# State tables and products in 64x64 blocks with later tables, and a 512-column product in the MLP's up units

## Chip, cores and metric

One core of one Trainium2 chip. The metric is the time of one execution on the device in microseconds (us); for the kernel before it is the median of three runs.

## The reference, cut to what matters

Two layers of a decoder trunk, one sequence of 256 tokens, model width 1024, all in float32.

```python
for l in range(DEPTH):                       # DEPTH = 2
    h = rmsnorm(x, norm_mix[l])
    u, sq, sk, sv, dq, dk, dv, gate_logits = jnp.split(h @ w_in[l], split_idx, axis=-1)
    y_ssm = jax.nn.gelu(s5_ssm(u, ...))      # 32 groups of 16 channels, 64 complex states each
    glu_a, glu_b = jnp.split(y_ssm @ ssm_w_glu[l], 2, axis=-1)
    y_ssm = glu_a * jax.nn.sigmoid(glu_b)
    ...                                      # stick-breaking and differential attention
    x = x + jnp.sum(gates * proj, axis=2) @ w_out[l]
    ...                                      # cross-attention into 256 memory tokens
    hm = rmsnorm(x, norm_mlp[l])
    x = x + jnp.square(jax.nn.relu(hm @ w_up[l])) @ w_down[l]      # hidden 4096

def s5_ssm(u, lam_re, lam_im, log_dt, b_re, b_im, c_re, c_im, d_skip):
    dt = exp(log_dt); lam_bar = exp(lam * dt); b_bar = (lam_bar - 1) / lam * b
    states = associative_scan(lam_bar, b_bar @ ug)      # over the 256 tokens
    return Re(c @ states) + d_skip * ug
```

## The kernel before, in words

**Weights.** All weights pass once, in 312 chunks of 128x1024 (512 KB), 156 a layer. SP loads them in order into seven slots; the load of chunk c waits until TensorE is done with chunk c - 7 (`load_chunk`). ScalarE copies each chunk to `w_hi` in the reduced type (L898, four slots), VectorE subtracts it from the original to `w_lo` (L1295, seven slots). A product is three matmuls that accumulate in PSUM (`three`, L1819 to L1821): high x high, high weight x low activation, low weight x high activation.

**Units.** Two chunks are a unit (`plan`): `u` 0 and 1, `sq` 2 and 3, `sk` 4 and 5, `sv` 6 and 7, `dq`, `dk`, `dv` 8 to 13, twelve gate units 14 to 25, then `glu`, `branch`, `wout`, cross-attention, and the MLP: `up` g (two units of 256 hidden columns), then `down` g-1. Kind "T" units keep the weights in the array and stream 256 columns of activations (48 matmuls); kind "N" units stream 512 columns of weights (24 matmuls). `unit_banks` gives each its PSUM banks; an `up` unit has one, T0 or T1, with its two blocks of 128 hidden columns side by side. ScalarE then takes the bank with relu, VectorE squares it, ScalarE and VectorE split it into `bT_hi`, `bT_lo` (`evac`).

**The order.** `side_stages` is a table written by hand: which other stages come after which unit. Every engine walks through units and stages in this same order and does its part; VectorE and ScalarE evacuate unit u, prepare the chunks of unit u + 2 (`prep`, before or after the stages by `DVE_PREP_EARLY` and its like), do `stage`, and last `later`. So an operation late on one of them holds all behind it.

**The state space.** 2048 states are 16 tiles (`STILES`) of 128 partitions; each tile has two groups of 64. Time is cut into 64 blocks of 4 steps. POOL (`tables`) makes powers of lam_bar (`product`, many operations on 128x16), zeroes the cross parts of `bN0` and `bN` (`zero_b`), and builds the phases in six doubling steps, then the decays. ScalarE gives the sine and cosine (`p_cos`), VectorE the reduced angle. VectorE multiplies them into C (`p_cv`) and B (`p_b0`, `p_bv`); because the two groups of a tile lie on different columns of a 128x128 block, the last sum of each runs once for each half of the partitions. TensorE makes `kt` from `bN0` and `ct` (`p_k`, L1931, and L1934 for the skip term), ScalarE copies it out in sixteen copies of 32 partitions; TensorE transposes `bN` (`p_bt`, L1804) and ScalarE copies it to `bt`. `p_k` follows unit 5, `p_bt` units 6 to 8. The input `u` is scaled by VectorE, goes to HBM and comes back turned (`turn_u`, at chunks 8, 10 and 12 of SP's order; the last part waits for `lam_made`). Then four times: `ssm_in` (TensorE L1963 into one bank, then eleven operations on VectorE with a scan), from unit 9 on (`FIRST`), and two units later `ssm_out` (L1977 and L1979, 128x128 weights, 64 columns). GELU follows at unit 15, its split at 18; `glu` (unit 26) needs it.
The tables of layer 1 are made in the same way beside layer 0's MLP, in `qk`, with the banks X0, X1.

**Beside it** run stick-breaking attention (`sb_s`, `sb_u`, `sb_p`, units 6 to 14, banks X0, X1, A3; matmuls on 64-row tiles at L1996 and L1998) and differential attention (`da_s`, `da_t`, `da_p`, from unit 16). For the first norm of layer 0 the kernel loads x transposed in two halves (`load_x_t`) and scales the result by the norm's factor afterwards (`row`, `r_row`), so the first products need no statistics.

## Time and profile before

| | |
|---|---|
| median of three runs | 1094.41 us (1093.07 to 1097.61) |
| profiled execution, its own time | 1096.48 us |
| its span | 1094.8 us, 18335 instructions |
| mean granted TensorE clock | 0.985 |
| HBM read | 172.87 MB |

The span is from the first to the last recorded instruction; the time has what lies around it too. An engine's busy time is the union of its instructions. A matmul's record is its latency: the next one starts long before it ends, so the distance between starts is what counts. In a timeline row, "x16" means that sixteen like instructions follow each other, and the second number is what they last together; in square brackets stands how long the engine was idle before, and what ended it.

### The profile page before, as it was taken

How to read it: one execution, taken by the hardware profiler on the slowest of the kernel's cores; microseconds unless marked ns; L12 is line 12 of the kernel's file. 1: busy time of each engine (PE TensorE's matmuls, PEld its weight loads, DVE VectorE, ACT ScalarE, POOL GpSimd, SP SyncE). 2: the span in 40 equal slices, each digit the busy share in tenths (PEclk: the TensorE clock that was granted, in tenths of full speed). 3: DMA queues.
4: the chain of work that ended last, by engine and by line, in shares of the span. 5: the costliest groups of instructions: out<-in, count | busy, mean ns of one | idle time of the engine just before them, and what ended most of it. 6: DMA issues, size and time to landing. Idle time of an engine off the chain costs nothing. (4 is left out here: it accounts for less than half of the span.)

```text
span 1094.8 us, 18335 instructions
## 1 busy us (share of the span) xinstructions
PE 1029.5 (94%) x7096; PEld 937.9 (86%) x7096; DVE 736.7 (67%) x1061; ACT 573.4 (52%) x868; POOL 176.7 (16%) x304
## 2 busy tenths in 40 slices
PE   5778999999999899999989999999999989999996
PEld 4766889989998799988979878998998979899995
DVE  4884975878875565887465579478787647555554
ACT  6446445546765555546554454554637546444442
POOL 5993300000000003997000011000000000000000
PEclk9889999999999999999999999999999999999998
DMA  7253336645554366654556543465565445666661
GB/s 281 97 173 95 98 120 194 201 141 174 176 175 149 96 232 182 189 172 136 172 173 189 163 130 97 135 213 154 155 181 175 146 135 160 190 189 192 182 188 74
DMA packets 58022, 177.21 MB, mean 162 GB/s; under 512 B 14160, under 2 KB 16208, under 8 KB 57680
## 3 DMA queue, kind: packets, MB, share of 16 engines
q1 hardware_dynamic: 57792, 176.04, 52.2%
q8 instruction: 57, 0.93, 0.3%
q14 instruction: 29, 0.24, 0.1%
q10 hardware_dynamic: 144, 0.00, 0.0%
HBM read 172.87 MB, written 3.15 MB: 161 GB/s over the span
## 5 line engine op out<-in xcount | busy, mean ns | idle before, releaser
L1295 DVE TENSOR_TENSOR s_w_lo<-s_raw,s_w_hi 128x1024 fp32r<-128x1024 f32 x312 | 377.3, 1238 | 146.7 <-ACT s_w_hi L898 143.0
L898 ACT ACTIVATE s_w_hi<-s_raw 128x1024 fp32r<-128x1024 f32 x312 | 321.0, 1054 | 215.2 <-PE p_T L1821 130.5
L1819 PE MATMUL p_T<-s_hT_hi,s_w_hi 128*128 128x256 f32 x1088 | 313.4, 288 | 12.0 <-DVE s_w_lo L1295 11.9
L1820 PE MATMUL p_T<-s_hT_lo,s_w_hi 128*128 128x256 f32 x1088 | 310.0, 285 | 0.0
L1821 PE MATMUL p_T<-s_hT_hi,s_w_lo 128*128 128x256 f32 x1088 | 309.7, 285 | 0.0
L1819 PEld LDWEIGHTS p_T<-s_hT_hi,s_w_hi 128*128 128x128 f32 x1088 | 210.7, 194 | 17.6 <-issue 16.2
L1820 PEld LDWEIGHTS p_T<-s_hT_lo,s_w_hi 128*128 128x128 f32 x1088 | 210.8, 194 | 0.4
L1821 PEld LDWEIGHTS p_T<-s_hT_hi,s_w_lo 128*128 128x128 f32 x1088 | 210.9, 194 | 0.0
L1819 PE MATMUL p_A<-s_w_hi,s_bT_hi 128*128 128x512 f32 x320 | 125.2, 391 | 2.4 <-DVE s_bT_lo L1295 2.4
L1820 PE MATMUL p_A<-s_w_lo,s_bT_hi 128*128 128x512 f32 x320 | 124.7, 390 | 0.0
L1821 PE MATMUL p_A<-s_w_hi,s_bT_lo 128*128 128x512 f32 x320 | 124.6, 389 | 0.0
L1819 PEld LDWEIGHTS p_A<-s_w_hi,s_bT_hi 128*128 128x128 f32 x320 | 60.1, 188 | 15.2 <-issue 3.2
L1821 PEld LDWEIGHTS p_A<-s_w_hi,s_bT_lo 128*128 128x128 f32 x320 | 60.1, 188 | 12.7
L1820 PEld LDWEIGHTS p_A<-s_w_lo,s_bT_hi 128*128 128x128 f32 x320 | 60.1, 188 | 11.7
L727 POOL TENSOR_TENSOR s_small<-s_small 128x16 f32<-128x16 f32 (+1 forms) x130 | 59.8, 483 | 10.2 <-ACT s_small L898 7.8
L1819 PE MATMUL p_T<-s_w_hi,s_hT_hi 128*128 128x512 f32 x128 | 52.2, 408 | 8.0 <-issue 8.0
L898 ACT ACTIVATE s_bT_hi<-s_att 128x512 fp32r<-128x512 f32 x32 | 20.2, 632 | 58.5 <-DVE s_att L1295 58.5
L1821 PE MATMUL p_T<-s_w_hi,s_hT_lo 128*128 128x512 f32 x128 | 50.8, 397 | 0.0
L1820 PE MATMUL p_T<-s_w_lo,s_hT_hi 128*128 128x512 f32 x128 | 50.7, 396 | 0.0
L727 POOL TENSOR_TENSOR s_small<-s_col,s_small 128x16 f32<-128x16 f32 x4 | 1.2, 313 | 296.7 <-ACT s_small L898 296.7
L1819 PE MATMUL p_A<-s_hT_hi,s_w_hi 128*128 128x256 f32 x128 | 37.8, 295 | 9.5 <-DVE s_hT_lo L1394 9.5
L1819 PE MATMUL p_T<-s_bT_hi,s_w_hi 128*128 128x256 f32 x160 | 45.9, 287 | 0.3 <-issue 0.3
(263 smaller groups left out, 1685.5 us busy)
## 6 DMA issues: line engine op xcount, KB each, us to landing
s_raw<-in_weights SPq DMA_DIRECT2D x312, 512.0 KB, 3.6
s_bt<-in_mem_t SPq DMA_DIRECT2D x2, 1024.0 KB, 6.1
s_st_y<-in_x_t SPq DMA_DIRECT2D x2, 512.0 KB, 6.9
s_x<-in_x SPq DMA_DIRECT2D x1, 1024.0 KB, 10.6
s_vN<-in_ssm_bc SPq DMA_DIRECT2D x2, 512.0 KB, 8.9
u_turn<-s_st_y SPq DMA_DIRECT2D x4, 256.0 KB, 3.8
s_uB<-u_turn SPq DMA_DIRECT2D x8, 128.0 KB, 3.4
s_bt<-in_mem SPq DMA_DIRECT2D x1, 1024.0 KB, 5.9
```

The lines of the kernel that those rows point to most:

```text
L727: return nc.gpsimd.tensor_tensor(o, i0, i1, op)
L898: return nc.scalar.activation(o, i, f, **kw)
L1295: return V.tensor_tensor(o, i0, i1, op)
L1819: mm(o, lhi, rhi, start=first, stop=False, **kw)
L1820: mm(o, lhi, rlo, start=False, stop=False, **kw)
L1821: return mm(o, llo, rhi, start=False, stop=last, **kw)
```

## The change

- `up` units: the high and low parts of the activations lie side by side in one tile `hT`. The high weight block streams both in one product of 512 columns into a whole bank, and the low weight block adds its 256 columns to the first half. A unit has two banks, T0 and T1 or X0 and X1. ScalarE copies the second halves, VectorE adds the first halves, and relu and square become one operation of VectorE.
- State space: each group has its own 64x64 block. `bt`, `ct`, `kt` are 64 columns wide; all their products are done as two products, on rows 0 to 63 and 64 to 127. The last sums of `p_cv`, `p_b0`, `p_bv` are one operation over all partitions; `bN` needs no zeroes. `p_bt` uses plain products with the identity in place of transposes. `p_k` has two products where one was (64 and 48 columns), and `kt` is copied in eight copies.
- Tables: POOL makes all angles in one operation, VectorE reduces them, ScalarE takes sine and cosine of all (also those of the rotary embedding); POOL makes the factors in fewer, wider operations. The phases are made by VectorE (`p_ph`), in units 9 to 11.
- Order in layer 0: the angles come before the statistics of the norm, which move behind unit 0; `row` moves behind unit 2. The tables begin two units later, the state stages at unit 13 (`FIRST`; 12 in layer 1). `turn_u` moves to chunks 16, 17 and 24, with eight transfers for four. x arrives in three parts. The memory tokens come later, and their transposed copy once instead of twice.

```diff
-FIRST = [9, 9]
+FIRST = [13, 12]
...
-    after(-1, "stats", "mix", 0)
-    after(-1, "stats", "mix", 1)
     if l == 0:
         after(-1, "p_angle", 0)
         after(-1, "p_cos", 0)
-        after(2, "lam", 0)
-        after(3, "lam", 1)
-        after(4, "p_params", 0)
-    after(1, "row")
+    for half in range(2):
+        after(-1 if l else 0, "stats", "mix", half)
+    if l == 0:
+        after(2, "put_u")
+        after(3, "lam_sum")
+        after(4, "lam_exp")
+        after(5, "lam")
+        after(13, "p_params", 0)
+    after(1 if l else 2, "row")
...
-        for n in range(8):
-            after(u["bt"][n // 2], "p_bt", tgt, n)
+        for n in range(4):
+            after(u["bt"][n], "p_bt", tgt, n)
+        for k in range(TAB_STEPS):
+            after(u["ph"][max(0, k - 3)], "p_ph", tgt, k)
     if l == 0:
-        pre(0, dict(ct=0, cv=(1, 2), b0=3, bv=(4, 5), k=(5, 6), bt=(6, 7, 7, 8)))
+        pre(0, dict(ct=-1, cv=(3, 4), b0=5, bv=(6, 8), k=(6, 7), bt=(8, 8, 10, 10), ph=(9, 10, 11)))
-        pre(1, dict(ct=up0 + 10, cv=(up0 + 12, up0 + 13), b0=up0 + 15, bv=(up0 + 16, up0 + 18),
-                    k=(up0 + 20, up0 + 21), bt=(up0 + 22, up0 + 23, up0 + 24, up0 + 25)))
+        pre(1, dict(ct=up0 + 10, cv=(up0 + 12, up0 + 13), b0=up0 + 14, bv=(up0 + 16, up0 + 17),
+                    ph=(up0 + 18, up0 + 19, up0 + 20), k=(up0 + 20, up0 + 21),
+                    bt=(up0 + 24, up0 + 25, up0 + 28, up0 + 29)))
...
-DVE_PREP_EARLY = set(range(0, 5)) | set(range(AT_UNIT["up", 0, 0], NU))
+DVE_PREP_EARLY = set(range(0, 6)) | set(range(AT_UNIT["up", 0, 0], NU))
...
-        return ["T0", "T1"][key[2]:][:1]
+        return ["T0", "T1"] if key[2] == 0 else ["X0", "X1"]
...
-        hT_hi, hT_lo = sb("hT_hi", [P, KD, T], F32R), sb("hT_lo", [P, KD, T], F32R)
+        hT = sb("hT", [P, KD, 2, T], F32R)
+        hT_hi, hT_lo = hT[:, :, 0, :], hT[:, :, 1, :]
...
-                    if c in (8, 10, 12):
-                        turn_u(l, c // 2 - 4, st)
+                    if c in (16, 17, 24):
+                        turn_u(l, (16, 17, 24).index(c), st)
...
-                    if l == 0 and c == 2 * AT_UNIT[("gate", 2), 0]:
+                    if l == 0 and c == 2 * AT_UNIT[("gate", 0), 0]:
                         sp.wait_ge(*st.at(s_ready, KB))
                         load(mem_raw, a["mem"][0].rearrange("(t p) d -> p t d", p=P), rows_landed)
-                    if c == 2 * AT_UNIT[("gate", 0), 0]:
-                        sp.wait_ge(*st.at(s_ready, KB))
-                        load(mem_t, a["mem_t"], mem_landed)
+                        load(mem_t[:, :, :], a["mem_t"], mem_landed)
...
+            nc.gpsimd.memset(kt[:, :, :], 0.0).then_inc(zeroed, 1)
+            nc.gpsimd.memset(bN0[:, :, :, :], 0.0).then_inc(zeroed, 1)
...
-            nc.gpsimd.memset(ct[:, :, :, :], 0.0).then_inc(zeroed, 1)
-            nc.gpsimd.memset(kt[:, :, :], 0.0).then_inc(zeroed, 1)
...
+                tt(TH[:, 1:1 + TAB_STEPS, :], TH[:, 0:1, :].broadcast_to([P, TAB_STEPS, STILES]),
+                   consts[:, 0:TAB_STEPS].unsqueeze(2).broadcast_to([P, TAB_STEPS, STILES]))\
+                    .then_inc(*st.sig(theta_ready, t + 1))
...
+                        for i, part in enumerate(X_PARTS):
+                            if i != 1:
+                                prep_chunk(i // 2)
+                            act.wait_ge(*st.at(xt_landed[i], 1))
...
-                    for q in (2 * n, 2 * n + 1):
-                        for j in range(BL):
-                            rows = slice(32 * j, 32 * j + 32)
-                            ins = fn(every[rows, q, :, 32 * j:P], src[32 * q:32 * q + 32, :, 0:P - 32 * j])
-                            last = n and q == 3 and j == BL - 1
-                            ins.then_inc(*st.sig(*freed(l, b, use))) if last else ins.then_inc(*st.mid())
+                    every = kt[:, :, :].rearrange("p (m e) c -> p e m c", e=2)
+                    for h in range(2):
+                        o = PC * h
+                        src = bank[b][o + 32 * n:o + 32 * n + 32, :].rearrange("p (m c) -> p m c", c=PC)
+                        fn(every[o:o + 32, n, :, :], src).then_inc(*st.mid())
+                        ins = fn(every[o + 32:o + 64, n, :, 32:PC], src[:, :, 0:32])
+                        ins.then_inc(*st.sig(*freed(l, b, use))) if n and h else ins.then_inc(*st.mid())
...
-                        take(r_b[i], b[0], key, ACT.Relu)
+                        act.wait_ge(*st.at(chunk_done, 2 * u + 2))
+                        for j, bk in enumerate(b):
+                            ins = fn(r_b[i][:, j * T:j * T + T], bank[bk][:, T:2 * T])
+                            ins.then_inc(*st.sig(up_copied)) if j else ins.then_inc(*st.mid())
...
+                        if s in (("p_angle", 0), ("p_cos", 0)):
+                            prep_chunk(2 + (s[0] == "p_cos"))
+                            n_first = AHEAD
...
+                    reduce_angle(st, TH[:, 0:n, :], KK[:, 0:n, :], THR[:, 0:n, :])
+                    V.tensor_scalar(THR[:, 0:n, :], THR[:, 0:n, :], PI_SAFE, -PI_SAFE, ALU.min, ALU.max)\
+                     .then_inc(*st.sig(angle_ready))
...
+                def products(raw, r, f, n, o):
+                    q = [o[:, 1024 * i:1024 * i + n * STILES * GC].rearrange("p (n i c) -> p n i c", n=n, c=GC) for i in range(2)]
+                    for i, m in enumerate((r, 1 - r)):
+                        tt(q[i], raw[:, m, :, :].unsqueeze(1).broadcast_to([P, n, STILES, GC]),
+                           FACTORS[:, i, f:f + n, :].unsqueeze(3).broadcast_to([P, n, STILES, GC])).then_inc(*st.mid())
+                    dve.wait_ge(*st.mine())
+                    return q
...
+                    q = products(c_raw, r, 0, BL - 1, early(t))
+                    tt(ct[:, r, :, GC:PC].rearrange("p i (n c) -> p n i c", c=GC), q[0], q[1],
+                       ALU.subtract if r else ALU.add).then_inc(*st.sig(ct_ready))
...
+                    q = products(b_raw, r, 3, BL, st_y[:, :, :].rearrange("p r n -> p (r n)"))
+                    tt(bN[:, r].rearrange("p i j c -> p j i c"), q[0], q[1], ALU.add if r else ALU.subtract)\
+                        .then_inc(*st.sig(bv_ready))
...
-                    for h in range(2):
-                        rows = slice(STATES * h, STATES * h + STATES)
-                        o = ct[rows, r, :, :].rearrange("p i (n h c) -> p n i h c", n=BL, h=2)[:, 1:BL, :, h, :]
-                        ins = tt(o, q[0][rows], q[1][rows], ALU.subtract if r else ALU.add)
...
+                    n = 1 << k
+                    c = [TURN[:, r, 1 + k, :].unsqueeze(1).unsqueeze(3).broadcast_to([P, 2, STILES, n]) for r in range(2)]
+                    e, o = phase[:, :, :, 0:n], phase[:, :, :, n:2 * n]
+                    part = st_y[:, :, :].rearrange("p r n -> p (r n)")[:, 0:2 * STILES * n]\
+                        .rearrange("p (r i n) -> p r i n", r=2, n=n)
+                    tt(o, e, c[0]).then_inc(*st.mid())
+                    tt(part, e, c[1]).then_inc(*st.mid())
                     dve.wait_ge(*st.mine())
...
+                    tt(o[:, 0], o[:, 0], part[:, 1], ALU.subtract).then_inc(*st.mid())
+                    tt(o[:, 1], o[:, 1], part[:, 0], ALU.add).then_inc(*(st.sig(phase_ready) if k + 1 == TAB_STEPS else st.mid()))
...
-                        dve.wait_ge(*st.at(*freed(l, b[0], key)))
-                        tt(q_b[i], r_b[i], r_b[i]).then_inc(*st.sig(sq_made))
+                        dve.wait_ge(*st.at(up_copied, 2 * g + i + 1))
+                        for j, bk in enumerate(b):
+                            tt(r_b[i][:, j * T:j * T + T], r_b[i][:, j * T:j * T + T], bank[bk][:, 0:T], ALU.add)\
+                                .then_inc(*st.sig(*freed(l, bk, key)))
+                        dve.wait_ge(*st.mine())
+                        V.scalar_tensor_tensor(out=q_b[i], in0=r_b[i], scalar=0.0, in1=r_b[i], op0=ALU.max, op1=ALU.mult)\
+                         .then_inc(*st.sig(sq_made))
...
+                                if key[0] == "up":
+                                    o = bank[banks[ft]]
+                                    mm(o[:, :], wh[:, k, c], hT[:, ks, :, :].rearrange("p r n -> p (r n)"),
+                                       start=(half == 0 and k == 0), stop=False, skip_group_check=True)
+                                    ins = mm(o[:, 0:T], wl[:, k, c], hi[:, ks, :], start=False,
+                                             stop=(half == 1 and k == kt // 2 - 1), skip_group_check=True)
+                                    continue
...
+                        tiles = [(e, slice(PC * h, PC * h + PC), slice(PC * h + 32 * e, PC * h + 32 * e + 32), PC * h)
+                                 for e in range(2) for h in range(2)]
+                        for m in range(STILES // 2):
                             for r in range(2):
-                                for q in range(4):
-                                    mm(bank[b][c * q:c * q + c, n * P:n * P + P], bN0[:, r, 4 * n + q, :],
-                                       ct[:, r, 4 * n + q, :], start=(r == 0), stop=False, skip_group_check=True)
-                            for q in range(4):
-                                ins = mm(bank[b][c * q:c * q + c, n * P:n * P + c], ident[0:c, 0:c],
-                                         diag_d[:, 4 * n + q, :], start=False, stop=True, skip_group_check=True)
+                                for e, rows, out_rows, p in tiles:
+                                    mm(bank[b][out_rows, PC * m:PC * m + PC], bN0[rows, r, 2 * m + e, GC:3 * GC],
+                                       ct[rows, r, 2 * m + e, :], start=(r == 0), stop=False, skip_group_check=True)
+                                for e, rows, out_rows, p in tiles:
+                                    mm(bank[b][out_rows, PC * m + GC:PC * m + PC], bN0[rows, r, 2 * m + e, 0:2 * GC],
+                                       ct[rows, r, 2 * m + e, 0:PC - GC], start=False, stop=False, skip_group_check=True)
+                            for e, rows, out_rows, p in tiles:
+                                two = slice(p, p + 2 * GC)
+                                ins = mm(bank[b][out_rows, PC * m:PC * m + 2 * GC], ident[two, two],
+                                         diag_d[two, 2 * m + e, :], start=False, stop=True, skip_group_check=True)
...
+                        for q in range(8):
+                            for h in range(2):
+                                rows = slice(PC * h, PC * h + PC)
+                                ins = mm(bank[b][rows, q * PC:q * PC + PC],
+                                         bN[rows, r, 8 * k + q, :, :].rearrange("p j c -> p (j c)"), ident[rows, rows],
+                                         start=True, stop=True, skip_group_check=True)
...
-                                ins = mm(bank[b][:, c + 1:c + NB], bt[:, r, i, :], uB[:, i, 0:NB - 1],
-                                         start=True, stop=True)
+                                for rows in HALVES:
+                                    ins = mm(bank[b][rows, c + 1:c + NB], bt[rows, r, i, :], uB[rows, i, 0:NB - 1],
+                                             start=True, stop=True, skip_group_check=True)
...
-                                mm(bank[b][:, c:c + NB], ct[:, r, i, :], st_y[:, r, i * NB:i * NB + NB],
-                                   start=(r == 0), stop=False)
-                            ins = mm(bank[b][:, c:c + NB], kt[:, i, :], uB[:, i, :], start=False, stop=True)
+                                for rows in HALVES:
+                                    mm(bank[b][rows, c:c + NB], ct[rows, r, i, :], st_y[rows, r, i * NB:i * NB + NB],
+                                       start=(r == 0), stop=False, skip_group_check=True)
+                            for rows in HALVES:
+                                ins = mm(bank[b][rows, c:c + NB], kt[rows, i, :], uB[rows, i, :], start=False, stop=True,
+                                         skip_group_check=True)
```

## Rows read from the trace of the kernel before

**Rows 1.** The page, busy us, share of the span and instructions of each engine

```profile
PE 1029.5 (94%) x7096; PEld 937.9 (86%) x7096; DVE 736.7 (67%) x1061; ACT 573.4 (52%) x868; POOL 176.7 (16%) x304
```

**Rows 2.** Timeline of PE in layer 0's MLP: start, length, instruction

```profile
455.04 0.39 PE L1821 MATMUL p_A<-s_w_hi,s_bT_lo 128*128 128x512 f32 x1
455.27 0.28 PE L1819 MATMUL p_T<-s_hT_hi,s_w_hi 128*128 128x256 f32 x1
...
457.66 0.28 PE L1821 MATMUL p_T<-s_hT_hi,s_w_lo 128*128 128x256 f32 x1
```

**Rows 3.** Stretches: length, busy PE, PEld, DVE, ACT, POOL, granted clock, DMA share, GB/s

```profile
9.45:13.10 3.65, 3.65 (x17) 3.65 (x18) 3.19 (x7) 3.62 (x8) 0.64 (x3) 1.00 1.03 421
9.45:95.36 85.91, 64.15 (x476) 57.77 (x477) 62.06 (x98) 45.56 (x80) 68.85 (x130) 0.88 0.44 159
...
514.90:518.30 3.40, 3.40 (x18) 3.40 (x18) 2.88 (x3) 1.54 (x3) 0.19 (x2) 0.51 0.00 0
950.00:1050.00 100.00, 100.00 (x628) 90.80 (x627) 55.77 (x54) 47.08 (x55) 0.00 (x0) 1.00 0.62 189
```

**Rows 4.** Timeline of PE: products that waited, in layer 0

```profile
29.75 0.55 PE L1819 MATMUL p_T<-s_hT_hi,s_w_hi 128*128 128x256 f32 x1 [6.51 <-DVE s_w_lo L1295]
...
70.43 0.77 PE L1819 MATMUL p_T<-s_w_hi,s_hT_hi 128*128 128x512 f32 x1 [7.13 <-issue]
...
88.53 1.65 PE L2005 MATMUL p_X<-s_att,s_tri 128*128 128x384 f32 x2 [3.07 <-DVE s_att L1713]
...
513.47 0.74 PE L1804 MATMUL p_X<-s_ident,s_gates 128*128 128x128 f32 x5 [1.90 <-ACT s_kt L898]
```

**Rows 5.** Timeline of PE: products on part of the array, transposes, state products

```profile
60.16 0.64 PE L1931 MATMUL p_A<-s_ct,s_tmp 128*32 128x128 f32 x16
60.73 0.26 PE L1934 MATMUL p_A<-s_att,s_ident 32*32 32x32 f32 x8
60.93 0.64 PE L1931 MATMUL p_A<-s_ct,s_tmp 128*32 128x128 f32 x16
...
102.34 0.39 PE L1998 MATMUL p_X<-s_qk 64*128 64x128 f32 x4
102.66 1.09 PE L1804 MATMUL p_A<-s_ident,s_gates 128*128 128x128 f32 x8
...
132.00 0.61 PE L1977 MATMUL p_A<-s_st_y,s_ct 128*128 128x64 f32 x4
```

**Rows 6.** Groups by line and shape, PE: counts, busy us, mean ns

```profile
L1977 PE MATMUL p_A<-s_st_y,s_ct 128*128 128x64 f32 x128 | 19.5, 275 | 0.0
L1963 PE MATMUL p_A<-s_uB,s_bt 128*128 128x63 f32 x128 | 15.6, 275 | 0.0
...
L1979 PE MATMUL p_A<-s_uB,s_kt 128*128 128x64 f32 x64 | 12.4, 275 | 0.0
L1804 PE MATMUL p_A<-s_ident,s_gates 128*128 128x128 f32 x32 | 4.4, 276 | 1.5 <-ACT s_bt L898 1.5
```

**Rows 7.** Timeline of DVE between 28 and 71 us

```profile
28.30 2.46 DVE L1295 TENSOR_TENSOR s_w_lo<-s_raw,s_w_hi 128x1024 fp32r<-128x1024 f32 x2 [3.99 <-ACT s_w_hi L898]
...
31.31 2.15 DVE L1295 TENSOR_TENSOR s_st_y<-p_A,s_r_row 128x512 f32<-128x512 f32 x2
...
39.02 1.83 DVE L1295 TENSOR_TENSOR s_att<-s_vN,s_small 128x768 f32<-128x768 f32 x2 [3.23 <-POOL s_small L727]
40.88 1.94 DVE L1295 TENSOR_TENSOR s_ct<-s_att 64x768 f32<-64x768 f32 x2
...
64.32 2.69 DVE L1295 TENSOR_TENSOR s_att<-s_vN,s_small 128x1024 f32<-128x1024 f32 x2
67.04 2.56 DVE L1295 TENSOR_TENSOR s_gates<-s_att 64x1024 f32<-64x1024 f32 x2
69.63 0.69 DVE L1535 SCALAR_TENSOR_TENSOR s_qk<-p_T,s_r_row 128x512 f32<-128x512 f32 x1
```

**Rows 8.** Timeline of ACT in layer 0's MLP

```profile
509.71 3.61 ACT L898 ACTIVATE s_kt<-p_X 32x512 f32<-32x512 f32 x8
```

More of the change, by code:

```diff
@@ L469, in hybrid_trunk @@
         x_landed = counted("x_landed", 1, step=16)
-        xt_landed = [counted(f"xt_landed{i}", 1, step=16) for i in range(2)]
+        xt_landed = [counted(f"xt_landed{i}", 1, step=16) for i in range(3)]
         lam_landed = counted("lam_landed", 1, step=16)
@@ L771, in product @@
-                def product(o, f, g, n):
-                    part = [small[:, 29 + 2 * i:29 + 2 * i + n, :] for i in range(4)]
-                    tt(part[0], f[0], g[0]).then_inc(*st.mid())
-                    tt(part[1], f[1], g[1]).then_inc(*st.mid())
-                    tt(part[2], f[0], g[1]).then_inc(*st.mid())
-                    tt(part[3], f[1], g[0]).then_inc(*st.mid())
-                    pool.wait_ge(*st.mine())
-                    tt(o[0], part[0], part[1], ALU.subtract).then_inc(*st.mid())
-                    tt(o[1], part[2], part[3], ALU.add).then_inc(*st.mid())
-                    pool.wait_ge(*st.mine())
@@ L1383, in row, with put_u @@
                     dve.wait_ge(*st.mine())
+                def put_u():
+                    dve.wait_ge(*st.at(chunk_done, 2 * AT_UNIT["u", 1] + 2))
+                    for i, bk in enumerate(("A0", "A2")):
+                        tt(by_block(u_flat[:, 512 * i:512 * i + 512]), by_place(bank[bk][:, :]),
+                           by_place(r_row[:, :]).broadcast_to([P, 2, BL, NB])).then_inc(*st.sig(*freed(l, bk, ("u", i))))
                 def norm(which):
@@ L1389, in norm @@
                     if which == "mix" and l == 0:
-                        for half in range(2):
-                            prep_chunk(half)
-                            for k in range(4 * half, 4 * half + 4):
+                        rope_angles()
+                        for i, part in enumerate(X_PARTS):
+                            if i != 1:
+                                prep_chunk(i // 2)
+                            for k in range(part.start, part.stop):
                                 dve.wait_ge(*st.at(norm_hi, k + 1))
@@ L1608, in stage @@
                         p_params(s[1])
-                    elif kind == "lam":
-                        lambdas(s[1])
+                    elif kind in ("lam_sum", "lam"):
+                        lambdas(kind)
+                    elif kind == "put_u":
+                        put_u()
+                    elif kind == "p_ct":
+                        p_ct(s[1])
                     elif kind == "mem_row":
```

402 lines of the change are left out of this document (155 added, 247 removed).

## The prediction

> **What bounds the kernel now.** The busy shares come first [rows 1]: TensorE works 94% of the span, VectorE 67%, so only what shortens TensorE's stream, or a wait inside it, counts. But a busy TensorE is a pipelined one: its matmuls are recorded as 280 to 390 ns long and start every 120 or 227 ns. So I price by the distance from one start to the next. In the MLP of layer 0 [rows 2] a 512-column product is followed after 0.23 us (0.227 over many), and from 455.27 to the twentieth 256-column product after it pass 2.39, 0.120 each. Then the stretches [rows 3]: from the first matmul at 9.45 us to 95.36 us, where unit 8 starts, the mean granted clock is 0.88 (2.4 GHz with windows at 1.2 GHz between), and in the MLP of layer 1 VectorE is busy 55.8 of 100 us under a full TensorE. Last the waits of that first stretch [rows 4]: 6.5 us before unit 2, 7.1 before unit 6, 3.1 before the first `sb_u`.
>
> The first stretch holds units 0 to 7: six with 48 products of 256 columns (6 x 48 x 0.120 = 34.6) and two with 24 of 512 (2 x 24 x 0.227 = 10.9), the `p_k` table (four groups of 0.77, 3.1 [rows 5]), and transposes, scores and the row product, about 5.5 at the same distances (an estimate). That is 54.1 of 85.9 us. The first 3.7 us run at a little under double distance (17 matmuls [rows 3]), 1.9 lost, which stays. So 29.9 us are stalls and half-clock work behind them. The rest of the kernel has few waits.
>
> **The change part by part.** Two facts price its products. A plain fp32 product is two instructions (the 32 products of L1979 in two layers are 64 there [rows 6]); a transpose is one. And a small product costs what its weights or its columns need: 128x128 weights with 64 columns start 0.112 apart (four last 0.61, one 0.275: 0.335 / 3), two tiles of 64 rows with 128 weight and 128 moving columns take 0.32 for four instructions (102.66 - 102.34) where the full array would need four times 0.109, sixteen instructions on four 32-column tiles take 0.57 together with a change of tile shape, and eight transposes last 1.09, one of them 0.33: 0.109 apart [rows 5].
>
> *MLP up products.* 16 units a layer, 16 blocks each, 512 blocks in all. Each replaces two 256-column products (0.240) by one of 512 (0.227): -6.8 us. The other end is 0, if the 256-column product that follows waits for its weights. TensorE loads one weight block less, but no row shows loads as the limit, so that adds nothing. ScalarE now copies half of each bank, VectorE adds the halves (at most 2 x 0.69 [rows 7] a unit, 32 units) and then squares: cost nothing, since VectorE has 44 of 100 us free there [rows 3], T0/T1 and X0/X1 come round only every fourth unit, and `down` reads a group two units later. Without that cover it would be 2 x 0.69 x 32 = 44 us at most.
>
> *State products* (`ssm_in`, `ssm_out`). Now 128 + 128 + 64 = 320 instructions [rows 6] at 0.112: 35.8 us. After: 640 on quadrants of 64x64. If the two diagonal quadrants run side by side, as the 64-row tiles in [rows 5] do, a pair has 64 weight and 64 moving columns, half of the 128 that cost 0.112: 320 x 0.056 = 17.9. Changes of tile shape come on top: of the 0.77 from 60.16 to 60.93 four sets of four tiles take 0.44 and two short identity sets 0.11, which leaves 0.1 for each of two changes; 16 stages with two each give 3.2. Sum -14.7; the other end, no overlap, is +3.2.
>
> *B tables* (`p_bt`). Now 32 transposes a layer [rows 6] at 0.109 (7.0 in all). After: plain products, so 256 instructions, 128 pairs: 7.2 and 1.2 for six changes there and back, +1.4. Without overlap +8.5.
>
> *K table* (`p_k`). Now 3.1 a layer. After: eight groups of 8 sets of four tiles (0.056 each), two identity sets (0.053) and two changes: 8 x 0.75 = 6.0. For two layers +5.8; with the two row halves one after the other 8 x 1.31, +14.8.
>
> *The start.* The causes [rows 4, 7]: `w_lo` of chunk 4 comes at 28.30, behind ScalarE, which stood in `p_cos` waiting for VectorE's angle, itself behind the norm statistics. Now the angles precede the statistics, so `w_hi` of chunks 4 and 5 should be there by 22 and `w_lo` by 23, about when unit 1 ends (22.6). The last sums of `p_cv` and `p_bv` ran twice over 64 partitions each (2.56 us for the two of `p_bv`, 1.94 of `p_cv`); now they run once over 128, so `p_bv` falls from 5.3 to 4.0 and `p_cv` from 3.8 to 2.8. POOL's table of phases becomes about 10 us of VectorE in units 9 to 11: per step two operations of 32 to 1024 columns and two of half of that, 1024 columns at 1.23 and the shortest at 0.2 (an estimate). SP's wait for `lam_made` with six weight chunks behind it goes from chunk 12 to chunk 24.
> I walked VectorE through units 2 to 13 with these durations. Unit 2 ends at 28.3, the row and unit 3 at 34.5, unit 4 at 40.3, unit 5 at 46.0. VectorE is by then behind: `put_u` 2.15, `lam` 0.9 (an estimate), both `p_cv` 5.6 and two preparations a unit put the evacuation of `sk1` at 47.9: stall 1.9, the new form of the 7.1. `p_b0` (3.8, by its columns) ends at 54.8, so `p_k` waits 1.4. Then `p_bv` stands ahead of `nl` in VectorE's queue: `sb_u` waits to 70.4, 2.9. Later units run without a wait: VectorE has 8 us of work a unit, TensorE 7 to 8. That is 6.2 of stalls, 3.5 for one or two half-clock windows behind them and 1.2 for what I missed: 10.9 of the 29.9 stay, so -19.0. Ends: 0 (each wait replaced) and -29.9. The first quarter of x lands earlier: -0.5.
> SP: `u_out` moves to chunks 16 and 17 and eight small transfers to 24; `uB` is needed at unit 13 (before 9), so nothing waits. The first `ssm_in` now wants the phases from VectorE, done near 111 by the walk, against 118.
>
> *Layer 0's MLP.* TensorE waits 1.9 at 513.5 for `kt`, which ScalarE writes in two runs of 3.6 us [rows 4, 8]; these fall to four wider copies in place of eight, so the wait goes. The half-clock window after it (3.4 us at 0.51 [rows 3]) costs 1.7. Together -3.6; other end 0.
>
> *Later state stages.* `ssm_in` (about 5 us of VectorE by its columns) now overlaps the first `da_s`, GELU the fourth: in the walk VectorE keeps just level, so I put +3; ends 0 and +8.
>
> Sum: -6.8 - 14.7 + 1.4 + 5.8 - 19.0 - 0.5 - 3.6 + 3.0 = -34.4. Against the profiled execution (1096.5, with a span of 1094.8) that is 1062.1; its time is 2.1 above the median of three, so 1060 on that scale, with an own range of 1047 to 1070.
>
> **Where a page speaks against it.** The rows show overlap for tiles of different rows writing to two banks (X0 and X1), and of different columns writing to one. None shows two row halves writing into one bank, which every new quadrant pair does. The Trainium skill, TensorEngine Tiling (Array Packing), section Restrictions and Gotchas, states that different row tiles cannot access the same PSUM bank at once. By it the first rival below holds.
>
> **The rivals.** *1. Row halves take turns,* because both write one bank. The three product terms become +3.2, +8.5 and +14.8 in place of -14.7, +1.4, +5.8: 34 more, 1094. For it: no row has this case, and the skill's sentence above. Against: the halves write different partitions, as the column tiles do that overlap in one bank. 0.17.
> *2. VectorE takes the place of every wait at the start.* It is busy 62 of 86 us there and gets the phases as well: the start term is 0, 1079. For it: my walk has it level with TensorE for ten units. Against: the tables' halved tails and the angles' new place. 0.16.
> *3. Slower: no tiles overlap at all.* Each quadrant instruction takes 0.056 alone: `p_k` becomes 8 x (32 x 0.056 + 8 x 0.053 + 0.2) = 19.3 a layer, +32.4; with 3.2 and 8.5 the products cost 44.1, against a gain of 26.9 elsewhere: 1112. It decides where the three terms together pass +26.9. Against: column tiles overlap in [rows 5]. 0.04.
> That the MLP product does not do what it says (term 0) is 1066, inside the range.
>
> **How the numbers follow.** Forecast 0.60, rival 2 0.16, rival 1 0.17, rival 3 0.04, mixtures nearer the old time 0.03. A measurement tells 0.5% (5.5 us) from no change. Faster: forecast, rival 2 and the part of rival 1 whose start gain is better than mine, 0.82. Same: the rest of rival 1 and mixtures, 0.12. Slower: rival 3 and rival 1 with a poor start, 0.06. Range 1046 to 1088: about 0.04 lies below it, and above it rival 3 and most of rival 1, about 0.16.
>
> **What would show it.** Right: in `ssm_out` two quadrant starts within 0.01 us and the next pair 0.056 later; the wait before unit 2 under 1 us; the first `sv` product by 50 us, unit 8 by 73; up products at 0.227 and 0.120; no wait on `kt` near 480 to 510. Rival 1: pairs 0.11 apart. Rival 2: TensorE waits for `w_lo` or for T banks between 30 and 75 us that sum to over 20. Wrong altogether: a new wait for `hid_ready` or the X banks in the MLP, or over 5 us in units 13 to 20.

## The result, and the profile after

| | before | after |
|---|---|---|
| median of 4 runs | 1093.99 us (1093.07 to 1097.61) | 1079.95 us (1078.63 to 1081.17) |
| ratio | | 0.9865, 95% interval 0.984 to 0.9891 |
| profiled execution, span | 1096.48, 1094.8 us | 1081.17, 1079.5 us |
| instructions | 18335 | 19185 |

The change is faster by 14 us. The forecast was 34.4: the direction is right, 1080 lies inside the range, but 20 us of the gain are missing. (1080 is also what rival 2 would give, but its mechanism is not there, as shown below.) The page's busy line against [rows 1]:

```profile
PE 1024.3 (95%) x7544; PEld 903.9 (84%) x7544; DVE 765.1 (71%) x1176; ACT 560.0 (52%) x863; POOL 47.2 (4%) x100
```

POOL's work moved to VectorE, which is busier by 28 us. Three stretches, the first from the first matmul to unit 8 as in [rows 3] (the columns are the same, the granted clock is the third from the right):

```profile
8.29:77.02 68.73, 60.62 (x677) 54.70 (x677) 48.96 (x78) 34.77 (x53) 10.45 (x27) 0.95 0.57 198
...
479.95:493.60 13.65, 11.37 (x325) 9.54 (x326) 11.83 (x16) 4.45 (x7) 0.00 (x0) 0.51 0.02 4
950.00:1050.00 100.00, 100.00 (x510) 84.72 (x509) 62.32 (x73) 48.34 (x65) 0.00 (x0) 1.00 0.57 189
```

The start takes 68.7 us instead of 85.9 and its granted clock is 0.95 instead of 0.88. The second row is new: 13.65 us at half clock in layer 0's MLP, where before there were 3.4 us.

Where the time went is best seen by setting the end of each unit on TensorE in one trace against the same unit in the other. The difference, after minus before, over four parts of the program (one profiled execution of each kernel, so the sum is not quite the 14.0 of the medians):

| part | forecast, from its terms | measured |
|---|---|---|
| layer 0 up to the MLP | -21.8 (start -19.5, state products -7.4, tables +3.6, late stages +1.5) | -18.8 |
| layer 0's MLP, with layer 1's tables | -3.4 (up -3.4, `kt` wait -3.6, tables +3.6) | **+8.8** |
| layer 1 up to the MLP | -5.9 (state products -7.4, late stages +1.5) | -3.8 |
| layer 1's MLP | -3.4 | -1.6 |
| sum | -34.4 | -15.3 |

12.2 of the 19.1 missing us are in one row. Within it one unit, `down` 4,1, ends its stretch 12.0 us later relative to the unit before it. Waits of TensorE in the new trace (in brackets the idle time and what ended it; "issue" means that the profile shows nothing it waited for):

```profile
28.51 0.35 PE L1775 MATMUL p_T<-s_hT,s_w_hi 128*128 128x256 f32 x1 [0.62 <-DVE s_w_lo L1224]
...
48.71 0.47 PE L1775 MATMUL p_T<-s_w_hi,s_hT 128*128 128x512 f32 x1 [2.70 <-issue]
...
60.01 0.26 PE L1902 MATMUL p_A<-s_tmp,s_ident 32*32 32x32 f32 x6 [1.09 <-issue]
...
63.74 0.25 PE L1895 MATMUL p_A<-s_ct,s_bN 64*32 64x64 f32 x3 [1.08 <-issue]
...
73.69 1.01 PE L1981 MATMUL p_X<-s_att,s_tri 128*128 128x384 f32 x1 [2.62 <-DVE s_att L1669]
...
215.99 0.44 PE L1760 MATMUL p_A<-s_ident,s_att 128*128 128x128 f32 x2 [3.11 <-DVE s_att L1681]
...
420.02 0.47 PE L1849 MATMUL p_X<-s_hT,s_w_hi 128*128 128x512 f32 x1 [0.74 <-DVE s_w_lo L1224]
...
482.23 0.44 PE L1895 MATMUL p_X<-s_ct,s_bN 64*32 64x64 f32 x8 [4.90 <-DVE s_att L1224]
```

The waits of 6.5 and 7.1 us of [rows 4] are now 0.62 and 2.70. The one at 482.23 is new, and it is what the prediction listed under "Wrong altogether", a wait for the X banks in the MLP: the K table of layer 1 waits for VectorE's write of `s_att`. That operation is no input of the table. It is the evacuation of up 5,1, which since the change sits in banks X0 and X1, and `p_k` asks for X0 one unit later. VectorE's timeline shows why it is late:

```profile
460.71 2.36 DVE L1224 TENSOR_TENSOR s_st_y<-s_dv,s_small 128x1024 f32<-128x1024 f32 x2
...
466.70 2.36 DVE L1224 TENSOR_TENSOR s_st_y<-s_dv,s_small 128x1024 f32<-128x1024 f32 x2
...
474.68 0.69 DVE L1224 TENSOR_TENSOR s_bT_lo<-s_att,s_bT_hi 128x512 fp32r<-128x512 f32 x1 [0.70 <-ACT s_bT_hi L848]
475.72 0.07 DVE L1406 MEMSET s_phase<- 128x16 f32 x1 [0.35 <-DVE s_bT_lo L1224]
...
478.99 0.49 DVE L1224 TENSOR_TENSOR s_phase<-s_phase,s_st_y 128x128 f32<-128x128 f32 x2
479.40 2.35 DVE L1224 TENSOR_TENSOR s_w_lo<-s_raw,s_w_hi 128x1024 fp32r<-128x1024 f32 x2
481.67 0.75 DVE L1224 TENSOR_TENSOR s_att<-s_att,p_X 128x256 f32<-128x256 f32 x2
```

Two `p_bv`, the first four phase steps (475.7 to 479.4) and a weight preparation stand ahead of the evacuation at 481.67. TensorE idles 4.9 us. Its granted clock falls to half about 2.4 us into that wait, and the K table runs at that rate: 9.3 us from its first to its last product, where e2 below has 6.8 at full clock.

### The profile page after: what moved, and what is told of

It is laid out like the page before. It is cut to its first block and busy times, and to the rows that moved or that the text cites. A ratio compares the mean times of both kernels' runs of the same rounds, so it can differ in the third digit from the quotient of the medians.

```text
span 1079.5 us, 19185 instructions
## 1 busy us (share of the span) xinstructions
PE 1024.3 (95%) x7544; PEld 903.9 (84%) x7544; DVE 765.1 (71%) x1176; ACT 560.0 (52%) x863; POOL 47.2 (4%) x100
## 5 line engine op out<-in xcount | busy, mean ns | idle before, releaser
L1224 DVE TENSOR_TENSOR s_w_lo<-s_raw,s_w_hi 128x1024 fp32r<-128x1024 f32 x312 | 373.3, 1227 | 115.1 <-ACT s_w_hi L848 110.8
L848 ACT ACTIVATE s_w_hi<-s_raw 128x1024 fp32r<-128x1024 f32 x312 | 320.5, 1054 | 184.4 <-PE p_T L1777 79.0
L1775 PE MATMUL p_T<-s_hT,s_w_hi 128*128 128x256 f32 x576 | 167.2, 290 | 0.6 <-DVE s_w_lo L1224 0.6
L1776 PE MATMUL p_T<-s_hT,s_w_hi 128*128 128x256 f32 x576 | 164.2, 285 | 0.0
L1777 PE MATMUL p_T<-s_hT,s_w_lo 128*128 128x256 f32 x576 | 164.1, 285 | 0.0
L1775 PEld LDWEIGHTS p_T<-s_hT,s_w_hi 128*128 128x128 f32 x576 | 111.8, 194 | 4.5 <-issue 3.4
L1776 PEld LDWEIGHTS p_T<-s_hT,s_w_hi 128*128 128x128 f32 x576 | 111.8, 194 | 0.1
L1777 PEld LDWEIGHTS p_T<-s_hT,s_w_lo 128*128 128x128 f32 x576 | 111.7, 194 | 0.0
L1849 PE MATMUL p_X<-s_hT,s_w_hi 128*128 128x512 f32 x256 | 91.3, 399 | 0.8 <-DVE s_w_lo L1224 0.7
L1849 PE MATMUL p_T<-s_hT,s_w_hi 128*128 128x512 f32 x256 | 91.3, 399 | 0.1
L1851 PE MATMUL p_X<-s_hT,s_w_lo 128*128 128x256 f32 x256 | 71.9, 281 | 0.0
L1851 PE MATMUL p_T<-s_hT,s_w_lo 128*128 128x256 f32 x256 | 71.9, 281 | 0.0
L848 ACT ACTIVATE s_bT_hi<-s_att 128x512 fp32r<-128x512 f32 x32 | 20.2, 632 | 85.2 <-DVE s_att L1550 85.2
L1849 PEld LDWEIGHTS p_X<-s_hT,s_w_hi 128*128 128x128 f32 x256 | 48.1, 188 | 13.2 <-issue 1.3
L1849 PEld LDWEIGHTS p_T<-s_hT,s_w_hi 128*128 128x128 f32 x256 | 48.1, 188 | 12.3 <-issue 0.5
L1775 PE MATMUL p_T<-s_w_hi,s_hT 128*128 128x512 f32 x128 | 52.2, 408 | 3.5 <-issue 3.5
```

The costliest lines, as they stand in the source:

```text
L848: return nc.scalar.activation(o, i, f, **kw)
L1224: return V.tensor_tensor(o, i0, i1, op)
L1775: mm(o, lhi, rhi, start=first, stop=False, **kw)
L1776: mm(o, lhi, rlo, start=False, stop=False, **kw)
L1777: return mm(o, llo, rhi, start=False, stop=last, **kw)
L1849: mm(o[:, :], wh[:, k, c], hT[:, ks, :, :].rearrange("p r n -> p (r n)"), start=(half == 0 and k == 0), stop=False, skip_group_check=True)
```

## The experiments

All ratios are against the kernel before, measured beside the run on the same chip; the changed kernel stands at 0.9865. Theory: the up units now share banks X0 and X1 with layer 1's tables, and VectorE, which frees them, is behind. Rival: VectorE's backlog alone, whatever asks for it, or the state tables alone.

**e1: K table one unit later.**

```diff
-                    k=(up0 + 20, up0 + 21),
+                    k=(up0 + 21, up0 + 22),
```

> The changed kernel with one edit in the order: layer 1's K table (p_k) is computed one unit later, after down 4,1 instead of after down 4,0. Theory (bank): p_k waits 4.9 us at 482 because it asks for bank X0 one unit after up 5,1 filled it; the half-clock stretch behind it takes the rest of the 12.0 us that this unit loses. One unit later the bank is free: the wait and the half-clock stretch go, about -12, 1068 us (1066 to 1071). Rival (VectorE's backlog): VectorE is about 5 us late at that point whatever asks for it, and the next thing that needs it (w_lo of the next chunks, hid_ready) waits instead: the time falls by less than 4, 1076 to 1080.

1086.91 us, ratio 0.9918 (0.9896 to 0.9941): slower than the changed kernel, which neither had said. The wait on X0 went, but three others came:

```profile
481.28 0.47 PE L1775 MATMUL p_A<-s_w_hi,s_bT_hi 128*128 128x512 f32 x1 [3.42 <-DVE s_w_lo L1224]
...
493.78 0.24 PE L1902 MATMUL p_X<-s_tmp,s_ident 32*32 32x32 f32 x2 [1.60 <-issue]
...
509.03 0.79 PE L1849 MATMUL p_X<-s_hT,s_w_hi 128*128 128x512 f32 x1 [6.55 <-ACT s_kt L848]
```

The first is the rival's: VectorE is late for the next weights too. The second is a stall inside the table (see e9). The last is the bank in the other direction. ScalarE copies the K table out in two parts (L848, `s_kt`):

```profile
496.31 2.00 ACT L848 ACTIVATE s_kt<-p_X 32x512 f32<-32x512 f32 x4 [6.58 <-PE p_X L1902]
...
506.97 2.00 ACT L848 ACTIVATE s_kt<-p_X 32x512 f32<-32x512 f32 x4
```

The second stands behind the evacuation of up 6,0, and up 6,1 waits for it. At the old place the table waits for the bank, one unit later the next up unit waits for the table: my expectation of -12 was wrong though the conflict is real. (e2 shows that the old place is good enough once VectorE is on time.) A step that is moved past one conflict has to be placed with its release, not only with its start.

**e2: phases of layer 1 four units later**, `p_k` left in its place.

```diff
-                    ph=(up0 + 18, up0 + 19, up0 + 20), k=(up0 + 20, up0 + 21),
+                    ph=(up0 + 22, up0 + 23, up0 + 24), k=(up0 + 20, up0 + 21),
```

> The changed kernel with the phases of layer 1 (p_ph) moved from the units after up 5,0, up 5,1 and down 4,0 to four units later each; p_k stays where it is. Theory (bank, with VectorE late because of 3.7 us of phases and two p_bv ahead): the evacuation of up 5,1 comes 3.7 us earlier, the wait of 4.9 falls to 1 or 2 and with it most of the half-clock stretch: -8 to -11, 1069 to 1072 us. If the phases are not what makes VectorE late, or if they make it late again at the later place: 1078 to 1081.

1070.83 us, ratio 0.9773 (0.9746 to 0.9799), inside the theory's bounds. The wait is down by 3.75, the length of the four phase steps:

```profile
478.67 0.32 PE L1895 MATMUL p_X<-s_ct,s_bN 64*32 64x64 f32 x8 [1.15 <-DVE s_att L1224]
```

Not all of the 9 us is this wait. By the unit ends of the two traces 6.1 us come back in layer 0's MLP. Another 4.0 lie in layer 1, 2.5 at its start and 1.5 in unit 25, where the changed kernel's trace has half-clock windows and this one has none. No run shows that the edit is their cause.

**e3: the up units in their old form.** `unit_banks` gives `["T0", "T1"][key[2]:][:1]` again; products, relu and square as before the change.

> The changed kernel with the up units as they were before: three products of 256 columns, banks T0 and T1 alone, relu by ScalarE, square by VectorE. It keeps everything of the state space. Theory (bank): the X0 conflict goes (-12.0), and the gain of the 512-column product is lost (0.107 us in each of 32 up units, +3.4): 1071 us (1069 to 1074). Rival (the late tables alone make the wait, not the up units' banks): 1080 + 3.4 = 1083.

1072.37 us, ratio 0.9785 (0.9762 to 0.9809), as the theory said. The larger half of the change, taken alone, is faster than the whole change. The edit takes away two things at once, the shared banks and two additions of VectorE in each up unit. The trace tells them apart in part:

```profile
477.10 0.32 PE L1879 MATMUL p_X<-s_ct,s_bN 64*32 64x64 f32 x8
...
479.20 0.69 DVE L1220 TENSOR_TENSOR s_att<-s_att 128x512 f32<-128x512 f32 x1
```

VectorE is late here too: it comes to up 5,1 (the square at 479.20) 7.8 us after that unit's last product starts, where it took 10.5 in the changed kernel. But the K table started 2.1 us before that, without a wait, since its bank is no longer VectorE's to free. So the backlog alone does not stop TensorE; it needs the shared bank.

**e4: the new up units alone**, on the kernel before.

> The kernel before with the new up units alone (512-column products in both parts, banks X0 and X1 for every second unit, the new evacuation). In it p_k of layer 1 stands two units after up 5,0, VectorE has the old tables beside it. Products: -0.107 x 32 = -3.4. Theory (bank): p_k after down 4,0 asks for X0 one unit after up 5,1 here too, but VectorE has no phases to make there, so the wait is small: 1088 to 1092. If the wait comes from the up units' new evacuation alone, it is here too: 1098 to 1103. My forecast of -6.8 would be 1087.

1111.86 us, ratio 1.0149 (1.0124 to 1.0174): slower than either end that I gave. I had counted one meeting on the X banks; the old tables give three. TensorE's waits:

```profile
481.32 0.47 PE L1906 MATMUL p_T<-s_hT,s_w_hi 128*128 128x512 f32 x1 [3.67 <-DVE s_w_lo L1303]
...
504.79 0.65 PE L1951 MATMUL p_X<-s_ct,s_tmp 128*32 128x128 f32 x16 [4.46 <-DVE s_att L1303]
...
526.79 0.77 PE L1906 MATMUL p_X<-s_hT,s_w_hi 128*128 128x512 f32 x1 [5.27 <-ACT s_bt L903]
...
538.30 1.06 PE L1817 MATMUL p_X<-s_ident,s_gates 128*128 128x128 f32 x8 [2.88 <-DVE s_att L1303]
```

Three of them are on X0 or X1, in both directions. Up to unit `down` 3,1 this kernel gains 0.10 to 0.11 us an up unit and nothing is lost; from there to the end of layer 0 it falls 16.5 us behind, where the tables of layer 1 use the same banks. The first is the weight preparation, late behind the new evacuation. So the change's two halves do not add: the MLP half is worth -3.4 by its products, and costs more than that by its banks and by VectorE's extra work, which this run does not part.

**e5: the GELU's split later.**

```diff
-    after(first + 9, "gelu_split")
+    after(24, "gelu_split")
```

> The changed kernel with one stage moved: gelu_split (the split of the GELU's result into its two parts, for glu after unit 25) stands after unit 24 in both layers, not after units 22 and 21. Theory: in the changed kernel its 1.29 us on VectorE stand at 208.6, ahead of the softmax of the next head, and the wait before the transposes at 216.0 is 3.11 us where it was 1.73, with a half-clock window behind it; with the stage moved the wait is 1.8 or less and the window goes: -2 to -5 over both layers, 1075 to 1078. Rival (the wait is VectorE's own chain for that head, whatever stands ahead): 1079 to 1081.

1074.97 us, ratio 0.981 (0.9792 to 0.9828), at the low end of the theory. The wait at 215.99 is the old size again:

```profile
216.49 0.44 PE L1760 MATMUL p_A<-s_ident,s_att 128*128 128x128 f32 x2 [1.72 <-DVE s_att L1681]
```

The unit in which it lies ends 2.88 us earlier in layer 0 and 2.07 in layer 1: 1.3 us of VectorE at the wrong place cost 5 us in this pair of traces. In layer 1, 1.5 of the 2.07 are a half-clock window behind a wait of 2.3 us, and six of the eight traces with that wait (e2, e3, e6 to e9) do not have the window, so about 3.4 us are the part that repeats.

**e6: the 512-column products first**, then those of 256 columns, in each column tile.

> The changed kernel, in all up units but up 0,0: the four 512-column products of a column tile first, then its four products of 256 columns, in place of 512, 256, 512, 256. In the changed kernel the starts after a 512-column product are 0.237 apart and those after a 256-column one 0.117, 0.354 for a pair, where I forecast 0.227 + 0.120 = 0.347. Theory (a change from 512 to 256 columns costs the 0.010): three of four pairs lose it, 0.227 comes back, -0.005 to -0.007 x 512 = about -2.6, 1077. Rival (512 columns of hT take 0.237 wherever they stand): 1080, and the trace shows 0.237 between two of them.

1079.12 us, ratio 0.985 (0.9831 to 0.9869): no difference that can be told. In the trace the starts are 0.232 and 0.1185 apart in place of 0.236 and 0.117. So neither reading holds fully: the mixed order costs 3 ns a pair (1.5 us in all), and 0.232 of a product on `hT` stays above the 0.227 of the MLP's `down` products.

**e7: statistics ahead of the angles again.**

> The changed kernel with layer 0's norm statistics ahead of the angles again, as before the change. Theory (the angles' place made the start's gain): ScalarE stands in p_cos again, w_hi and w_lo of chunk 4 are late, TensorE waits about 6 us before unit 2, +4 to +8, 1084 to 1088. Rival (the smaller tables on VectorE and their later place made it): the early wait is back, but the later ones shrink by as much, 1079 to 1081.

1085.56 us, ratio 0.9912 (0.989 to 0.9933), inside the theory's bounds. `w_lo` is late again, but for unit 1, one unit earlier than I said, and by 3.6 us, not 6:

```profile
20.75 0.36 PE L1775 MATMUL p_A<-s_hT,s_w_hi 128*128 128x256 f32 x1 [3.59 <-DVE s_w_lo L1224]
```

The angles' place is worth about 5 us: unit 1 ends 6.5 us later than in the changed kernel, and 5.4 of that is left at the end of layer 0. The rest of the start's gain comes from elsewhere, by the walk from the tables; no run tests that.

**e8: old up form in groups 5 to 7 only**, where the tables want X0 and X1.

> The changed kernel, with the up units of groups 5 to 7 in both layers in the old form (three products of 256 columns, banks T0 and T1, old evacuation); groups 0 to 4 keep the 512-column products. The tables of layer 1 want banks X0 and X1 only in groups 5 to 7. Theory (bank): as e3 (which stood at 1072.4) but with the 0.107 us of 20 of 32 up units: 1070 to 1071. Rival (e3's gain came from the lighter evacuation in groups 0 to 4 too, whose waits for w_lo at 420 and 454 add 1.8): 1072 to 1074.

1075.13 us, ratio 0.9807 (0.9784 to 0.983), above both ranges. The bank wait is gone and the waits for `w_lo` at 420 and 454 are still there, as the rival said. But a stall that the profile puts down to nothing came inside `p_k`, with half clock behind it:

```profile
482.85 0.33 PE L1910 MATMUL p_X<-s_tmp,s_ident 32*32 32x32 f32 x8 [2.06 <-issue]
```

**e9: the K table's products in two halves,** four groups behind one unit and four behind the next.

```diff
...
-                        for m in range(STILES // 2):
+                        for m in range(4 * s[2], 4 * s[2] + 4):
...
```

> The changed kernel with the K table's products in two halves: the first four of its eight groups where they were, the last four behind the next unit; ScalarE copies all of it after the second. Every run so far shows inside p_k, on TensorE, waits of 0.5 to 2.1 us that no semaphore explains ('issue'): 1.09 and 1.08 in the changed kernel, 2.06 in e8. Theory (supply): 640 short instructions 18 ns apart come faster than they are supplied; with half as many in one go the stalls vanish, -2 in layer 0; in layer 1 the evacuation of X0 comes a unit later, which leaves the bank wait as it is: 1076 to 1079. Rival (the stalls come with any long wait before them, not with the count): they stay, 1079 to 1082.

(The 640 instructions are those of both layers, a table has 320.) 1077.63 us, ratio 0.9844 (0.9829 to 0.9859), inside the theory's bounds, 2.3 below the changed kernel and not told apart from it by the intervals. In layer 0 one stall of 1.38 us is left of two of 1.09 and 1.08. Layer 1 has none, but its first half ran at half clock, where the unsplit table of layer 1 shows none either; e11 is the better test of it.

The traces say more about these stalls than the run does. They record the loads of instructions on a queue of their own, on the page of the changed kernel as (packets, MB, share of 16 engines)

```profile
q8 instruction: 61, 1.00, 0.4%
```

That is 61 packets of 16 KB for 15088 matmuls and weight loads of TensorE, 57 for 14192 in the kernel before: one for about 250 instructions in both. Two of the changed kernel's land at 58.78 and 62.27 us, and TensorE, which had stopped at 58.92 and 62.66, starts again at 60.01 and 63.74. The twelve traces with the new table have 23 such stalls inside `p_k`, 0.4 us and longer, and every one ends 1.2 to 1.6 us after a packet has landed. Packets that follow each other during a table start 3.3 to 5.2 us apart; in no trace are two closer. A group of 40 products is 80 instructions with the weight loads, so at 0.72 us a group TensorE uses up 250 in about 2.3 us, and at the 1.16 us of half clock in 3.6 (estimates from these rows). So at full clock the table outruns the loads, and at half clock it about keeps pace.

**e10 to e12: together.** e10 is e2 and e5; e11 adds e9's halves; e12 adds e6's order.

> The edits of e2 (phases of layer 1 later) and e5 (gelu_split after unit 24) together on the changed kernel. They lie in different stretches, so if each took away its own wait the gains add: 0.9773 / 0.9865 and 0.981 / 0.9865 give 0.9719 of before, 1065 us (1063 to 1068). If one of them only met the other's window, 1069 to 1071.

1067.89 us, ratio 0.9758 (0.9745 to 0.9771), 3 us above the sum, just inside its bounds. e2 and e5 each had one half-clock window less at the start of layer 1 (-2.45 us in both traces), which can go only once.

> e10 with the K table in two halves as in e9. If the supply theory holds, e10's stalls inside p_k (0.7 to 2 us in each layer) go and nothing takes their place: -1 to -3 against e10, 1062 to 1064. Otherwise as e10, or up to +3 where up 6,1 waits for X0 behind the later copies of kt.

1065.91 us, ratio 0.9733 (0.9718 to 0.9749), 2 us above the theory's bounds. In layer 1 the table's stall is gone. In layer 0 one is left, in the last of the first four groups, the same products at which the unsplit table stops first (60.01 above):

```profile
58.69 0.32 PE L1898 MATMUL p_A<-s_ct,s_bN 64*32 64x64 f32 x8
58.83 0.27 PE L1901 MATMUL p_A<-s_ct,s_bN 64*32 64x48 f32 x8
58.91 0.29 PE L1898 MATMUL p_A<-s_ct,s_bN 64*32 64x64 f32 x8
59.02 0.26 PE L1901 MATMUL p_A<-s_ct,s_bN 64*32 64x48 f32 x8
59.22 0.24 PE L1905 MATMUL p_A<-s_tmp,s_ident 32*32 32x32 f32 x2
60.19 0.26 PE L1905 MATMUL p_A<-s_tmp,s_ident 32*32 32x32 f32 x6 [0.73 <-issue]
```

> e11 with the grouped order of e6 (512-column products of a column tile first). e6's trace has 0.232 and 0.1185 for the two kinds where the changed kernel has 0.237 and 0.117: 0.003 a pair, -1.5 us in 512: 1061 to 1063, about what a measurement can tell.

1065.98 us, ratio 0.9743 (0.973 to 0.9756), 3 us above the bounds: the 1.5 us of e6's order do not show. The stall of layer 0 is 0.41 here; in layer 1 one of 0.86 has moved behind the second half, into up 6,0 (TensorE starts again at 486.72, 1.3 us after a packet lands). e10, e11 and e12 all beat the kernel before and the changed one. e11 and e12 can't be told apart, and the intervals of e11 and e10 overlap by a little, so the split's gain is not shown by the times.

## Why the prediction was right in direction and wrong in size

- **State products: right.** Forecast -14.7. From one start to the next they take 17.7 us in layer 0 before (7.1 `ssm_in`, 10.6 `ssm_out`) and 10.2 after, so -14.9 for both layers. A tile of `ssm_out` is six pairs:

```profile
141.51 0.40 PE L1951 MATMUL p_A<-s_st_y,s_ct 64*64 64x64 f32 x8
141.74 0.28 PE L1954 MATMUL p_A<-s_uB,s_kt 64*64 64x64 f32 x4
141.86 0.40 PE L1951 MATMUL p_A<-s_st_y,s_ct 64*64 64x64 f32 x8
```

  From 141.51 to 141.86 pass 0.35 us for twelve instructions, 0.058 a pair, against my 0.056. The two of a pair start 0.007 us apart. Rivals 1 and 3 fall with these rows. The Trainium skill, TensorEngine Tiling (Array Packing), section Restrictions and Gotchas, would have the two row halves take turns in one bank; this trace doesn't agree, both halves write bank A2 here and share their 0.058.
- **B and K tables: right, but for stalls.** `p_bt` takes 4.0 and 4.3 us (before 3.5 by the forecast's distances), +1.3 against +1.4. A group of `p_k` takes 0.72 against my 0.75. What I did not have are the stalls inside it, 2.2 us in layer 0. From unit end to unit end, with the changes of tile shape around it, `p_bt` costs 5.2 us in layer 0's MLP against 3.5 before, 1 us more than its term.
- **The start: right.** With the first matmul 1.2 us earlier and the stretch to unit 8 17.2 us shorter, 18.3 are gained by then. 24 of the old `p_bt` transposes stood in that stretch and now stand behind it (24 x 0.109 = 2.6), which leaves 15.7. The terms (-19.0, -0.5, +2.9 for `p_k`) give 16.6. Its waits are where the walk had them: 2.70 at 48.7 (walk: 1.9 at 47.9), 2.62 before the first `sb_u` (2.9), and unit 8 by 77 (73 was said). In part this is luck: the 1.4 before `p_k` are not in this trace, where a half-clock window made the unit before it longer (e5, without that window, has the wait, 1.31), and the stalls of 2.2 us inside `p_k`, which the walk did not have, take their place. Rival 2 falls: the waits between 30 and 75 us sum to 7.5, not 20.
- **MLP up products: half the size.** The 512-column product is followed after 0.236, not 0.227, the 256-column one after 0.117: 0.353 a block against 0.360. A unit ends 0.107 earlier, -3.4 us over 32 units, where the term was -6.8. I took the distance of a stream of equal products for one that alternates with a smaller one; e6 shows that the order makes 3 of the 6 ns that are missing a block.
- **The up units "cost nothing" beside VectorE: wrong, and the largest miss.** The step that failed is "T0/T1 and X0/X1 come round only every fourth unit", by which the sum put the evacuation at nothing. It holds among up units. X0 and X1 are also the banks of layer 1's tables, which are asked for one unit after an up unit has filled them. And "44 of 100 us free" is from layer 1's MLP; in layer 0's, where the tables are made, VectorE is nearly full even before the change. A stretch of the kernel before (19.70 of 20.80 us are VectorE's):

```profile
476.90:497.70 20.80, 19.01 (x149) 16.93 (x147) 19.70 (x17) 6.79 (x8) 20.33 (x18) 1.00 0.56 170
```

  The wait costs 4.9 us, the half clock behind it about 4.4 (12.0 less 4.9 and the 2.7 by which the K table is longer anyway), together 9.3 of the 12.2 missing in layer 0's MLP. Two waits for `w_lo` (0.9 us each in the units at 420 and 454) add 1.8, and the kernel before had one of 1.6 (at 485.6) that is gone. e2 (VectorE relieved) gives 6.1 us back in this part of the program, e3 (banks apart and VectorE relieved) 7.8, and e3's trace shows VectorE late without holding TensorE. e4 has the same meetings with the old tables: +16.6 in place of -3.4. No run shares the banks without giving VectorE the additions, so the price of the banks alone stays open.
- **The `kt` wait: right.** It is gone. Unit up 6,1 gains 4.5 us, of which 0.9 are the eight transposes that moved to later units and 0.1 the unit's own products; the rest is the 3.5 to 3.6 of the forecast.
- **Later state stages: undersized.** +3.0 was forecast, 2.9 and 2.1 us come in unit 25 alone, and e5 names the one operation that makes them (1.5 of the 2.1 by a half-clock window that does not always follow). The walk of VectorE stopped at unit 13, and FIRST moved `gelu_split` to unit 22.

What stays open: why the instruction packets come no closer than 3.3 us, and whether the stalls go when they do; their timing points to them, but no run changed the loading. And of layer 1's smaller miss, 1.1 us are a longer half-clock window at its start, which none of the other eleven traces with the new table has (3.4 us or none there, 6.8 in the changed kernel).

## What to carry to other kernels

A buffer's slack is to be counted over all its users in the stretch, not over the loop that the edit touches, and an engine's free time is to be read in that same stretch. Two edits can be worth less together than one alone; here the smaller saving (3 us) took banks that the tables use, and undoing it gave 8 us. When a wait on a shared buffer is mended by moving a step, look where its release lands (e1): moving other work off the engine that releases it (e2) was the repair that worked here.

## What the runs showed of the hardware

- **Two 64x64 quadrants on the diagonal run side by side into one bank**, 0.058 us a pair inside a stage and 0.064 over all 640 instructions with the changes of tile shape, against the 0.112 of one product on the whole array.
- **A long run of very short products outruns the loading of its instructions.** 320 products 18 ns apart (0.72 us for a group of 40) stall for 0.4 to 2.1 us at a time (1.09 and 1.08 in the changed kernel, 2.06 in e8, 1.60 in e1), and each of the 23 stalls ends 1.2 to 1.6 us after a 16 KB instruction packet lands. Where the whole table ran at half clock (layer 1 of the changed kernel, e5, e6 and e7, a group every 1.16 us) there is none; in layer 0 of e1 and e5 one of 0.5 falls into a half-clock window. In halves of 160, layer 1 has none inside the table (2.88 us each at full clock in e11 and e12), but e12 has one of 0.86 just behind it, and layer 0 keeps one of 0.4 to 1.4.
- **A product's distance depends on its neighbours:** 512 columns take 0.227 after each other in `down`, 0.232 on `hT` in e6, 0.236 alternating with 256 columns. A product of 256 columns is followed after 0.117 there, after 0.120 in a stream of its own.
- **Half-clock windows can double the price of a wait, and do not always come.** Within the wait of 4.9 us a stretch of 13.65 us at 0.51 began, and it cost about as much as the wait; with e2's 1.15 us the clock stayed whole. Of eight traces with the wait of 3.1 us before unit 25 of layer 0 seven have a window of 3.4 us there, and of the same eight, with 2.3 us in layer 1, two.
